# Local attention in a two-layer decoder trunk: counts of keys added to the mask as logarithms, sums of exponentials taken by ScalarE, one head of each pair scaled by VectorE

## The chip, the cores and the metric

The kernel runs on one core of one Trainium2 chip. The metric is the device time in microseconds (us); lower is better. The engines are TensorE (PE in the rows, PEld for its weight loads), VectorE (DVE), ScalarE (ACT), GpSimd (POOL) and SyncE (SP). ns is nanoseconds.

## The reference

Two layers, each with a hybrid token mixer, a cross-attention and a gated convolutional feed-forward part, on 256 tokens of width 1024. The change touches one part of the mixer, the dilated window attention of 8 heads of 64 columns:

```
DL_PATTERN = ((128, 1), (512, 4), (2048, 16))
def dilated_branch(q, k, v, window, dilation):
    ...
    s = jnp.where(valid, s, -jnp.inf)
    m = jnp.max(s, axis=-1, keepdims=True)
    p = jnp.exp(s - m)
    den = jnp.sum(p, axis=-1, keepdims=True)
    o = jnp.einsum('brhnqk,brhnkc->brhnqc', (p / den).astype(v.dtype), vw)
    lse = (m + jnp.log(den))[..., 0]
...
    wts = jax.nn.softmax(jnp.stack(lses, axis=-1), axis=-1)
    o = jnp.einsum('bshn,nbshc->bshc', wts, jnp.stack(outs, axis=0).astype(jnp.float32))
```

Three branches with different windows are merged by their softmax denominators. That merge equals one softmax over all keys in which a key that lies in n of the branches (n is 0, 1, 2 or 3) counts n times.

## The kernel before

The whole trunk is written out by hand, engine by engine; every engine runs its own list in order and the lists are tied by semaphores (`Signal` objects; `own.link` makes VectorE wait for its own last instruction). All weights pass through as 512 KB groups in a ring of four. ScalarE makes the high part of a group (`whi`, line 569), VectorE the low part (`wlo`, line 996), both in `split_group`; TensorE multiplies with both. `split(g)` means "all groups up to g". The numbers of the groups (`G_SBQK`, `G_SBV` and so on) give the order in which TensorE uses them.

Local attention comes as four pairs of heads, c = 0 to 3, r = 0 or 1 within a pair. Queries lie on the partitions: token tile 0 has 128 columns of keys and tile 1 has 256, so a head is a 128x128 piece and a 128x256 piece, 384 columns (`AW`) together. Its buffers are `sms[c % 2][r]`, those of even pairs in `arena`, those of odd pairs in `V`. The mask `negm` (0 or -3e38) and the counts `mult` (0 to 3) are 384 columns each in the constants `cst`, which are loaded once and serve both layers. The steps of a pair are:

1. TensorE, `dl_scores(c)` (lines 1796 and 1797): scores into the PSUM banks `psAB[r]`. Head r of pair c waits for `nb_ready` of head r of pair c - 1, because that is when the bank is free.
2. VectorE, `scores_max(c)` (lines 1235, 1237, 1240): adds the mask, copies the scores to `sms` and takes the row's maximum, a reduction that the trace shows as a custom instruction and an accumulator read for each piece; then the negated scaled maximum, which signals `nb_ready`.
3. ScalarE, `exp_pair(c)` (line 689): exponentials in place, signals `exp_done`.
4. VectorE, `probabilities(c)` (lines 1250, 1253): multiplies by `mult` with a running sum, then the reciprocal, which signals `den_ready`.
5. ScalarE, `scale_pair(c)` (line 698): multiplies both heads by the reciprocals, signals `p_ready`.
6. TensorE, `dl_flip(c)` (line 1598): transposes into `psCD`; ScalarE copies it out (`p_columns`, line 706), TensorE multiplies with the values (`dl_values`, lines 1808 and 1809).

TensorE's list puts one weight group between these steps, so its order around the change is: `dl_scores(0)`, group `G_SBQK`, `dl_scores(1)`, group `G_SBQK + 1`, `dl_flip(0)`, `dl_scores(2)`, group `G_SBQK + 2`, `dl_values(0)`, `dl_flip(1)`, `dl_scores(3)`, and so on. VectorE's list there is:

```
                split(G_DLV + 3 + AHEAD)
                dve.wait_ge(cst_in.sem, 16)
                scores_max(0)
                split(G_SBQK + AHEAD)
                probabilities(0)
                scores_max(1)
                split(G_SBQK + 1 + AHEAD)
                probabilities(1)
                scores_max(2)
```

Of the kernel before, what the change touches and what calls it, by code (L numbers as in the profile page):

```python
# [145 lines left out]
def hybrid_trunk(nc, x, mem, pos, consts, gains, params, pw, stream, out):  # L146
    with ExitStack() as ctx:
# [222 lines left out]
        den_ready = signal("den_ready", DL_HEADS)  # L370
        p_ready = signal("p_ready", DL_HEADS)
        p_tr = signal("p_tr", DL_HEADS)
# [48 lines left out]
        def st(i, n=1):  # L421
            return stat[:, i:i + n]
# [130 lines left out]
        def _(act):  # L553
# [54 lines left out]
            for l in range(DEPTH):  # L608
# [75 lines left out]
                def exp_pair(c):  # L684
                    for r in range(2):
                        act.wait_ge(nb_ready.sem, nb_ready.at(l, 2 * c + r + 1))
                        for q, (a, b) in enumerate(((0, P), (P, AW))):
                            p = sms[c % 2][r][:, a:b]
                            e = act.activation(p, p, ACT.Exp, bias=st(S_NB + 4 * (c % 2) + 2 * r + q),
                                               scale=HD ** -0.5)  # L690
                        e.then_inc(exp_done.sem, 1)

                def scale_pair(c):
                    for r in range(2):
                        act.wait_ge(den_ready.sem, den_ready.at(l, 2 * c + r + 1))
                        for q, (a, b) in enumerate(((0, P), (P, AW))):
                            p = sms[c % 2][r][:, a:b]
                            e = act.activation(p, p, ACT.Copy, scale=st(S_RDEN + 4 * (c % 2) + 2 * r + q))
                        e.then_inc(p_ready.sem, 1)

# [85 lines left out]
                exp_pair(0)  # L786
                scale_pair(0)
                split(G_SBQK + 1 + AHEAD)
                exp_pair(1)
                split(G_SBQK + 2 + AHEAD)  # L790
                p_columns(0)
                scale_pair(1)
                exp_pair(2)
                split(G_SBQK + 3 + AHEAD)
                mixed_hi(4, o_done, 1, attended)
                p_columns(1)
                scale_pair(2)
                exp_pair(3)
# [3 lines left out]
                transposed_in(sbT.rearrange("p c n -> p (c n)"), [a[:, :] for a in accs[0]], G_SBQK + PER_TILE, sbT_in)  # L802
                scale_pair(3)
                mixed_hi(6, o_done, 3, attended)
# [177 lines left out]
        def _(dve):  # L982
# [113 lines left out]
            for l in range(DEPTH):  # L1096
# [132 lines left out]
                def scores_max(c):  # L1229
                    w = 4 * (c % 2)  # L1230
                    for r in range(2):
# [4 lines left out]
                        for q, (a, b) in enumerate(((0, P), (P, AW))):  # L1236
# [4 lines left out]
                                          None, ALU.mult).then_inc(nb_ready.sem, 1)  # L1241

                def probabilities(c):

                    w = 4 * (c % 2)
                    for r in range(2):
                        dve.wait_ge(exp_done.sem, exp_done.at(l, 2 * c + r + 1))
                        for q, (a, b) in enumerate(((0, P), (P, AW))):
                            p = sms[c % 2][r][:, a:b]
                            e = dve.tensor_tensor_reduce(p, p, mult[:, a:b], 1.0, 0.0, ALU.mult, ALU.add,  # L1250
                                                         st(S_DEN + w + 2 * r + q))
                        own.link(e)
                        dve.reciprocal(st(S_RDEN + w + 2 * r, 2), st(S_DEN + w + 2 * r, 2)).then_inc(den_ready.sem, 1)

                def mixed_lo(n, chunk, src, bias=None):
# [114 lines left out]
                split(G_DLV + 3 + AHEAD)  # L1370
                dve.wait_ge(cst_in.sem, 16)
                scores_max(0)
                split(G_SBQK + AHEAD)
# [217 lines left out]
        def _(pe):  # L1591
# [44 lines left out]
            for l in range(DEPTH):  # L1636
# [162 lines left out]
                def dl_flip(c):  # L1799
                    for r in range(2):  # L1800
                        pe.wait_ge(p_ready.sem, p_ready.at(l, 2 * c + r + 1))
                        flip(psCD[r], sms[c % 2][r], 3).then_inc(p_tr.sem, 1)
# [452 lines left out]
```

## Time and profile before

| | |
|---|---|
| median of 3 runs | 817.45 us (816.84 to 817.47) |
| the profiled execution | 817.97 us, of which span 815.8 us from first to last instruction |
| PE busy | 807.4 us, 99% |
| DVE busy | 653.9 us, 80% |
| ACT busy | 528.3 us, 65% |
| POOL busy | 29.3 us, 4% |
| TensorE's granted clock | 1.000 (full speed) |

Shares are of the span. Matmuls overlap in the trace and their ends are modelled, so two neighbouring PE rows are best compared by their starts. Local attention lies at about 72 to 104 us in the first layer and 470 to 503 us in the second.

### The profile page before, as it was taken

How to read it: one execution, taken by the hardware profiler on the slowest of the kernel's cores; microseconds unless marked ns; L12 is line 12 of the kernel's file. 1: busy time of each engine (PE TensorE's matmuls, PEld its weight loads, DVE VectorE, ACT ScalarE, POOL GpSimd, SP SyncE). 2: the span in 40 equal slices, each digit the busy share in tenths (PEclk: the TensorE clock that was granted, in tenths of full speed). 3: DMA queues.
4: the chain of work that ended last, by engine and by line, in shares of the span. 5: the costliest groups of instructions: out<-in, count | busy, mean ns of one | idle time of the engine just before them, and what ended most of it. 6: DMA issues, size and time to landing. Idle time of an engine off the chain costs nothing.

```text
span 815.8 us, 12147 instructions
## 1 busy us (share of the span) xinstructions
PE 807.4 (99%) x4636; PEld 698.2 (86%) x4636; DVE 653.9 (80%) x1149; ACT 528.3 (65%) x823; POOL 29.3 (4%) x54
## 2 busy tenths in 40 slices
PE   8999999999999999999999999999999999999997
PEld 5998888889888888888899889888998888888885
DVE  6899996778776899997387999948788489999753
ACT  5656886567657777765365589756767477776441
POOL 2100000010010000000010000001000000000000
PEclk9999999999999999999999999999999999999999
DMA  8765345472574465556666453456635545655651
GB/s 300 285 180 182 96 137 168 143 258 95 168 242 141 157 205 204 179 187 218 193 205 231 151 155 104 136 175 204 209 114 196 181 130 181 202 174 191 231 182 52
DMA packets 40446, 145.72 MB, mean 179 GB/s; under 512 B 4594, under 2 KB 4738, under 8 KB 40388
## 3 DMA queue, kind: packets, MB, share of 16 engines
q1 hardware_dynamic: 38448, 138.38, 52.1%
q0 software_dynamic: 1936, 6.55, 2.3%
q8 instruction: 37, 0.61, 0.3%
q14 instruction: 21, 0.17, 0.1%
q10 hardware_dynamic: 4, 0.00, 0.0%
HBM read 143.87 MB, written 1.05 MB: 178 GB/s over the span
## 4 chain that ended last, share of the span: by engine, by line
PE 96%; DVE 2%; issue 1%; ACT 1%; DMA 0%; DVEq 0%; POOLq 0%; POOL 0%; ACTq 0%
PE acc L1685 8%; PE acc L1651 5%; PE acc L1652 5%; PE acc L1653 5%; PE psCD L1685 4%; PE acc L1695 4%; PE acc L1668 4%; PE acc L1748 4%; PE psAB L1685 4%; PE acc L1750 4%; PE acc L1749 4%; PE acc L1669 3%; PE acc L1670 3%; PE psAB L1651 3%; PE psAB L1652 3%; PE psAB L1653 3%
## 5 line engine op out<-in xcount | busy, mean ns | idle before, releaser
L996 DVE TENSOR_TENSOR wlo<-raw,whi 128x1024 fp32r<-128x1024 f32 x240 | 288.0, 1222 | 68.3 <-ACT whi L569 66.7
L569 ACT ACTIVATE whi<-raw 128x1024 fp32r<-128x1024 f32 x240 | 249.7, 1058 | 119.4 <-PE acc L1653 43.6
L1685 PE MATMUL acc<-xT,whi 128*128 128x512 f32 x288 | 89.0, 390 | 0.0
L1685 PEld LDWEIGHTS acc<-xT,whi 128*128 128x128 f32 x288 | 54.1, 188 | 11.8
L1539 DVE SCALAR_TENSOR_TENSOR KT<-V,par,KT 128x255 f32<-128x255 f32 (+1 forms) x144 | 60.0, 480 | 2.1 <-ACT KT L929 1.5
L1695 PE MATMUL acc<-xT,wlo 128*128 128x256 f32 x288 | 58.0, 283 | 0.0
L1276 DVE SCALAR_TENSOR_TENSOR arena<-arena,par 128x256 f32<-128x256 f32 x120 | 50.3, 482 | 0.8 <-ACT arena L769 0.8
L1668 PE MATMUL acc<-xT,whi 128*128 128x256 f32 x176 | 50.9, 289 | 0.0
L1685 PE MATMUL psCD<-xT,whi 128*128 128x512 f32 x160 | 50.0, 393 | 0.0
L1669 PE MATMUL acc<-xT,whi 128*128 128x256 f32 x176 | 49.7, 283 | 0.0
L1670 PE MATMUL acc<-xT,wlo 128*128 128x256 f32 x176 | 49.7, 282 | 0.0
L496 POOL TENSOR_TENSOR stat<-stat 128x1 f32<-128x1 f32 x30 | 18.8, 628 | 771.5 <-DVE stat L1136 400.7
L1695 PEld LDWEIGHTS acc<-xT,wlo 128*128 128x128 f32 x288 | 44.8, 191 | 0.0
L1685 PE MATMUL psAB<-xT,whi 128*128 128x512 f32 x128 | 39.7, 391 | 0.0
L929 ACT ACTIVATE KT<-V,par 128x256 f32<-128x256 f32 x72 | 37.4, 596 | 0.6 <-DVE V L1525 0.6
L1668 PEld LDWEIGHTS acc<-xT,whi 128*128 128x128 f32 x176 | 33.6, 191 | 2.9 <-issue 2.7
L619 ACT ACTIVATE junk<-acc 128x512 bf16<-128x512 f32 x20 | 11.8, 592 | 37.0 <-PE acc L1769 22.5
L1651 PE MATMUL psAB<-whi,gT 128*128 128x512 f32 x88 | 34.2, 389 | 0.0
L1652 PE MATMUL psAB<-wlo,gT 128*128 128x512 f32 x88 | 34.2, 389 | 0.0
L1653 PE MATMUL psAB<-whi,gT 128*128 128x512 f32 x88 | 34.2, 389 | 0.0
L1669 PEld LDWEIGHTS acc<-xT,whi 128*128 128x128 f32 x176 | 33.7, 191 | 0.1
L1670 PEld LDWEIGHTS acc<-xT,wlo 128*128 128x128 f32 x176 | 33.6, 191 | 0.0
(336 smaller groups left out, 2084.0 us busy)
## 6 DMA issues: line engine op xcount, KB each, us to landing
raw<-stream_dram SPq DMA_DIRECT2D x256, 512.0 KB, 4.2
gpost<-gain_dram POOLq DMA_DIRECT2D x6, 512.0 KB, 5.2
gpre<-gain_dram POOLq DMA_DIRECT2D x5, 512.0 KB, 5.9
memn<-mem_dram SPq DMA_DIRECT2D x2, 512.0 KB, 10.0
out_dram<-h SPq DMA_DIRECT2D x4, 256.0 KB, 2.1
cst<-const_dram SPq DMA_DIRECT2D x1, 896.0 KB, 6.3
h<-x_dram SPq DMA_DIRECT2D x2, 256.0 KB, 3.0
h<-x_dram SPq DMA_DIRECT2D x1, 512.0 KB, 7.4
```

The source lines that it names most:

```text
L569: act.activation(home(g)[0], raw[:, s * GW:(s + 1) * GW], ACT.Copy).then_inc(w_hi.sem, 1)
L996: dve.tensor_tensor(lo, raw[:, cols], hi.bitcast(F32), ALU.subtract).then_inc(w_lo.sem, 1)
L1276: e = dve.scalar_tensor_tensor(acc, src, w, acc, ALU.mult, ALU.add)
L1539: e = dve.scalar_tensor_tensor(y[:, c, shift:SEQ], u[:, 0:SEQ - shift], par[:, PC_FW + 3 * fc + 1 - k:PC_FW + 3 * fc + 2 - k], y[:, c, shi ...
L1651: pe.matmul(outs[t], a_hi, whi[:, cols], start=k == 0, stop=False)
L1652: pe.matmul(outs[t], a_hi, wlo[:, cols], start=False, stop=False)
L1653: e = pe.matmul(outs[t], a_lo, whi[:, cols], start=False, stop=k == k_of - 1)
L1668: pe.matmul(dst, whi[:, cols], hi[:, toks], start=k == 0 and c % 2 == 0, stop=False)
L1669: pe.matmul(dst, whi[:, cols], lo[:, toks], start=False, stop=False)
L1670: e = pe.matmul(dst, wlo[:, cols], hi[:, toks], start=False, stop=k == KC - 1 and c % 2 == 1)
L1685: e = pe.matmul(up_halves(j, c), whi[:, cols], both, start=k == 0, stop=k == KC - 1)
L1695: e = pe.matmul(up_halves(j, c)[:, 0:SEQ], wlo[:, cols], hi, start=False, stop=False)
```

## The change

The counts leave the work of every pair. In the first layer only, before the first maximum, VectorE turns the counts into 8 times their logarithm (8 undoes the score scale) by a quadratic through 0 at count 1, and adds this to the mask `negm`. From then on the exponential itself holds the count. ScalarE sums the exponentials as it makes them (`accum_out`), VectorE takes only the reciprocals, ScalarE scales head 0 of a pair and VectorE scales head 1. `p_ready` becomes two signals.

```diff
@@ ScalarE
                             p = sms[c % 2][r][:, a:b]
-                            e = act.activation(p, p, ACT.Exp, bias=st(S_NB + 4 * (c % 2) + 2 * r + q),
-                                               scale=HD ** -0.5)
+                            n = 4 * (c % 2) + 2 * r + q
+                            e = act.activation(p, p, ACT.Exp, bias=st(S_NB + n), scale=HD ** -0.5,
+                                               accum_out=st(S_DEN + n))
                         e.then_inc(exp_done.sem, 1)
...
-                def scale_pair(c):
-                    for r in range(2):
-                        act.wait_ge(den_ready.sem, den_ready.at(l, 2 * c + r + 1))
-                        for q, (a, b) in enumerate(((0, P), (P, AW))):
-                            p = sms[c % 2][r][:, a:b]
-                            e = act.activation(p, p, ACT.Copy, scale=st(S_RDEN + 4 * (c % 2) + 2 * r + q))
-                        e.then_inc(p_ready.sem, 1)
+                def scale_first(c):
+                    act.wait_ge(den_ready.sem, den_ready.at(l, 2 * c + 1))
+                    for q, (a, b) in enumerate(((0, P), (P, AW))):
+                        p = sms[c % 2][0][:, a:b]
+                        e = act.activation(p, p, ACT.Copy, scale=st(S_RDEN + 4 * (c % 2) + q))
+                    e.then_inc(p0_ready.sem, 1)
@@ VectorE
+                def log_counts():
+
+                    two, three = float(HD ** 0.5 * np.log(2.0)), float(HD ** 0.5 * np.log(3.0))
+                    bend = three / 2 - two
+                    rise = sms[1][0]
+                    own.link(dve.tensor_scalar(rise, mult, bend, two - 2 * bend, ALU.mult, ALU.add))
+                    own.link(dve.scalar_tensor_tensor(rise, mult, -1.0, rise, ALU.add, ALU.mult))
+                    own.link(dve.tensor_tensor(negm, negm, rise, ALU.add))
+
                 def probabilities(c):
 
                     w = 4 * (c % 2)
                     for r in range(2):
                         dve.wait_ge(exp_done.sem, exp_done.at(l, 2 * c + r + 1))
-                        for q, (a, b) in enumerate(((0, P), (P, AW))):
-                            p = sms[c % 2][r][:, a:b]
-                            e = dve.tensor_tensor_reduce(p, p, mult[:, a:b], 1.0, 0.0, ALU.mult, ALU.add,
-                                                         st(S_DEN + w + 2 * r + q))
-                        own.link(e)
                         dve.reciprocal(st(S_RDEN + w + 2 * r, 2), st(S_DEN + w + 2 * r, 2)).then_inc(den_ready.sem, 1)
+                    dve.wait_ge(den_ready.sem, den_ready.at(l, 2 * c + 2))
+                    for q, (a, b) in enumerate(((0, P), (P, AW))):
+                        p = sms[c % 2][1][:, a:b]
+                        e = dve.tensor_scalar(p, p, st(S_RDEN + w + 2 + q), None, ALU.mult)
+                    e.then_inc(p1_ready.sem, 1)
...
                 dve.wait_ge(cst_in.sem, 16)
+                if not l:
+                    log_counts()
                 scores_max(0)
@@ TensorE
-                        pe.wait_ge(p_ready.sem, p_ready.at(l, 2 * c + r + 1))
+                        p_ready = p1_ready if r else p0_ready
+                        pe.wait_ge(p_ready.sem, p_ready.at(l, c + 1))
```

TensorE's list keeps its order. VectorE's and ScalarE's lists change at the places below (line numbers after the change are 1 to 12 higher; ISA is the custom instruction and its accumulator read).

VectorE in the first layer, ahead of the first maximum, before:

```order
L1276 SCALAR_TENSOR_TENSOR arena<-arena,par 128x256 x4
L996 TENSOR_TENSOR wlo<-raw,whi 128x1024
L1235 MEMSET stat 128x2
L1237 ISA arena,stat<-psAB,cst 128x128
L1237 ISA stat 128x1
```

and with the change:

```order
L1286 SCALAR_TENSOR_TENSOR arena<-arena,par 128x256 x4
L997 TENSOR_TENSOR wlo<-raw,whi 128x1024
L1249 TENSOR_SCALAR V<-cst 128x384
L1250 SCALAR_TENSOR_TENSOR V<-cst,V 128x384
L1251 TENSOR_TENSOR cst<-cst,V 128x384
L1236 MEMSET stat 128x2
```

Three instructions of 384 columns now stand between the last weight split and the first maximum. In the second layer this place is as before.

VectorE, the probabilities of pair 0 behind a weight split, before, head 0:

```order
L996 TENSOR_TENSOR wlo<-raw,whi 128x1024
L1250 ISA arena,stat<-arena,cst 128x128
L1250 ISA stat 128x1
L1250 ISA arena,stat<-arena,cst 128x256
L1250 ISA stat 128x1
L1253 RECIPROCAL stat<-stat 128x2
```

(the same five instructions follow for head 1, then the MEMSET of the next maximum) and with the change:

```order
L997 TENSOR_TENSOR wlo<-raw,whi 128x1024
L1258 RECIPROCAL stat<-stat 128x2 x2
L1262 TENSOR_SCALAR arena<-arena,stat 128x128
L1262 TENSOR_SCALAR arena<-arena,stat 128x256
L1236 MEMSET stat 128x2
```

Eight instructions went, two came, in each of the four pairs of both layers.

ScalarE, exponentials of head 1 and scaling of both heads of pair 0, before:

```order
L689 ACTIVATE arena<-arena,stat 128x128
L689 ACTIVATE arena<-arena,stat 128x256
L698 ACTIVATE arena<-arena,stat 128x128
L698 ACTIVATE arena<-arena,stat 128x256
L698 ACTIVATE arena<-arena,stat 128x128
L698 ACTIVATE arena<-arena,stat 128x256
L569 ACTIVATE whi<-raw 128x1024
```

and with the change:

```order
L691 ACTIVATE arena,stat<-arena,stat 128x128
L691 ACTIVATE arena,stat<-arena,stat 128x256
L699 ACTIVATE arena<-arena,stat 128x128
L699 ACTIVATE arena<-arena,stat 128x256
L570 ACTIVATE whi<-raw 128x1024
```

The exponentials have a second output (`stat`), and one head's scaling is gone.

## Rows read from the trace of the kernel before

**Rows 1.** The page: span and busy time of the engines.

```profile
span 815.8 us, 12147 instructions
...
PE 807.4 (99%) x4636; PEld 698.2 (86%) x4636; DVE 653.9 (80%) x1149; ACT 528.3 (65%) x823; POOL 29.3 (4%) x54
```

**Rows 2.** TensorE's waits: total us, times, longest; the longest of four rows.

```profile
PE acc L1623 <- POOL idle L499: 1.4, 1, 1.4
```

**Rows 3.** Timeline of TensorE, first layer: start, length, line.

```profile
72.65 0.50 PE L1796 MATMUL psAB<-arena 64*128 64x128 f32 x4
...
73.51 0.39 PE L1668 MATMUL acc<-xT,whi 128*128 128x256 f32 x1
...
76.58 0.53 PE L1796 MATMUL psAB<-arena 64*128 64x128 f32 x3
...
77.58 0.38 PE L1668 MATMUL acc<-xT,whi 128*128 128x256 f32 x1
...
80.56 0.82 PE L1598 MATMUL psCD<-cst,arena 128*128 128x128 f32 x6
81.31 0.50 PE L1796 MATMUL psAB<-arena 64*128 64x128 f32 x4
```

**Rows 4.** Timeline of VectorE, first layer.

```profile
74.81 0.06 DVE L1235 MEMSET stat<- 128x2 f32 x1
...
75.60 0.17 DVE L1240 TENSOR_SCALAR stat<-stat 128x2 f32<-128x2 f32 x1
...
76.51 0.17 DVE L1240 TENSOR_SCALAR stat<-stat 128x2 f32<-128x2 f32 x1
...
77.72 0.29 DVE L1250 CUSTOM_DVE_ANT_0 arena<-arena,cst 128x128 f32<-128x128 f32 x1
...
79.25 0.06 DVE L1235 MEMSET stat<- 128x2 f32 x1
...
80.95 0.17 DVE L1240 TENSOR_SCALAR stat<-stat 128x2 f32<-128x2 f32 x1
```

**Rows 5.** Timeline of TensorE, second layer.

```profile
474.71 0.49 PE L1796 MATMUL psAB<-arena 64*128 64x128 f32 x2
...
475.62 0.48 PE L1796 MATMUL psAB<-arena 64*128 64x128 f32 x2
...
476.47 0.38 PE L1668 MATMUL acc<-xT,whi 128*128 128x256 f32 x1
```

**Rows 6.** Timeline of VectorE, second layer; in brackets idle before it.

```profile
449.28 2.56 DVE L1276 SCALAR_TENSOR_TENSOR arena<-arena,par 128x256 f32<-128x256 f32 x6 [0.77 <-ACT arena L769]
...
475.40 0.17 DVE L1240 TENSOR_SCALAR stat<-stat 128x2 f32<-128x2 f32 x1
```

**Rows 7.** Timeline of VectorE at 36 us and 64 us: chains linked by semaphore.

```profile
36.90 0.23 DVE L1020 TENSOR_SCALAR arena<-arena 128x128 f32<-128x128 f32 x1
37.16 0.95 DVE L1026 SCALAR_TENSOR_TENSOR arena<-arena 128x128 f32<-128x128 f32 x3
...
64.81 0.42 DVE L1226 TENSOR_TENSOR arena<-arena 128x256 f32<-128x256 f32 x1
```

**Rows 8.** Groups by line and shape: busy us, mean ns | idle us before.

```profile
L1467 DVE TENSOR_SCALAR arena<-arena,stat 128x256 f32<-128x256 f32 x16 | 4.9, 351 | 0.3
L1293 DVE SCALAR_TENSOR_TENSOR arena<-arena 128x768 f32<-128x768 f32 x4 | 3.8, 958 | 1.9 <-ACT arena L723 1.9
...
L1036 DVE TENSOR_SCALAR xn<-memn,stat 128x1024 f32<-128x1024 f32 x2 | 1.5, 746 | 0.0
```

**Rows 9.** Timeline of ScalarE: attention pair 0, and cross-attention.

```profile
76.10 1.50 ACT L689 ACTIVATE arena<-arena,stat 128x128 f32<-128x128 f32 x4
78.59 1.55 ACT L698 ACTIVATE arena<-arena,stat 128x128 f32<-128x128 f32 x4 [0.99 <-DVE stat L1253]
...
190.44 0.47 ACT L855 ACTIVATE arena<-psAB,stat 128x256 f32<-128x256 f32 x1
190.79 0.20 ACT L855 ACTIVATION_READ_ACCUMULATOR arena<-psAB,stat 128x1 f32 x1
```

More of the change, by code:

```diff
@@ L370, in hybrid_trunk @@
         den_ready = signal("den_ready", DL_HEADS)
-        p_ready = signal("p_ready", DL_HEADS)
+        p0_ready = signal("p0_ready", DL_HEADS // 2)
+        p1_ready = signal("p1_ready", DL_HEADS // 2)
         p_tr = signal("p_tr", DL_HEADS)
@@ L786, in _ @@
                 exp_pair(0)
-                scale_pair(0)
+                scale_first(0)
                 split(G_SBQK + 1 + AHEAD)
@@ L791, in _ @@
                 p_columns(0)
-                scale_pair(1)
+                scale_first(1)
                 exp_pair(2)
@@ L796, in _ @@
                 p_columns(1)
-                scale_pair(2)
+                scale_first(2)
                 exp_pair(3)
@@ L802, in _ @@
                 transposed_in(sbT.rearrange("p c n -> p (c n)"), [a[:, :] for a in accs[0]], G_SBQK + PER_TILE, sbT_in)
-                scale_pair(3)
+                scale_first(3)
                 mixed_hi(6, o_done, 3, attended)
```

## The prediction

> **What bounds the kernel now.** I read the page first, then TensorE's waits, then the timelines of TensorE and VectorE side by side. The page shows TensorE busy for 807.4 of 815.8 us [rows 1], VectorE and ScalarE well below. The table of TensorE's waits has four rows only, the longest 1.4 us and at the very start of the program [rows 2]. So TensorE's own list is the time: work taken from VectorE or ScalarE buys nothing unless TensorE stands waiting for it, and whatever makes TensorE wait longer is added to the end in full, because nothing behind it is idle that could take it up.
>
> A wait shorter than a matmul's modelled length doesn't show as idle time, so I compared starts. The score products of a pair cost TensorE 0.86 us when nothing holds them: pair 0 starts at 72.65, the next weight group at 73.51 [rows 3]. Pair 1 of the first layer takes 1.00 us (76.58 to 77.58), and in the second layer 1.76 us (474.71 to 476.47), with head 1 starting only at 475.62 [rows 3, 5]. What holds it is VectorE: the instruction that frees the bank of head 1 ends at 475.40 + 0.17 = 475.57, 0.05 us before head 1 starts, and the next group follows 0.85 us after that start [rows 5, 6]. The first layer obeys the same sum: VectorE ends at 76.51 + 0.17 = 76.68, plus 0.05, plus 0.85, gives 77.58, and that is the row [rows 3, 4]. So in both layers TensorE already waits for VectorE at `dl_scores(1)`, by 0.14 us in the first and 0.90 us in the second. This is the one place of the attention where VectorE sets the end.
>
> **The change part by part.**
>
> *The logarithm of the counts.* Three VectorE instructions of 384 columns go in ahead of the first maximum, first layer only, each followed by a wait for itself. No row has 384 columns, so I go between rows. The TENSOR_SCALAR with constants took 0.23 us at 128 columns [rows 7]; the two rows with a scalar from memory, 351 ns at 256 and 746 ns at 1024 columns, give (746 - 351)/768 = 0.51 ns a column [rows 8]; 0.23 + 256 x 0.51 ns = 0.36 us. The SCALAR_TENSOR_TENSOR: three at 128 columns in 0.95 us with two gaps are 0.29 each [rows 7], and 958 ns at 768 columns [rows 8] gives 1.04 ns a column; 0.29 + 256 x 1.04 ns = 0.56 us. The TENSOR_TENSOR: 0.42 at 256 columns [rows 7], plus 128 x 1.04 ns = 0.55 us. The gap of a self-wait is 37.16 - 36.90 - 0.23 = 0.03 us [rows 7], three times 0.09. Sum: 0.36 + 0.56 + 0.55 + 0.09 = **1.56 us**. From below: 256 columns for all three, 0.35 + 0.42 + 0.42 + 0.09 = 1.28 us. From above: the first at 1.04 ns a column (0.50), the other two as long as the 768-column row (0.96 each), 0.09: 2.51 us. I take 1.56, since 384 columns lie far nearer to the rows at 256 than to that at 768.
>
> For this price there is a rule in the Trainium skill, page "VectorE: DVE Perf Modes", section on the TRN2 errata: an SBUF to SBUF operation takes 58 cycles plus columns divided by the mode's factor, at 0.96 GHz. By its figures the three would be an estimated 0.26, 0.46 and 0.46 us, 1.27 us with the gaps, and the time 818.7 us. The trace doesn't agree: a TENSOR_TENSOR of 256 columns took 0.42 us [rows 7] where that formula has 0.33. The same section's other formula, (N + 151) cycles, has 0.42 and agrees.
>
> *Who waits for it.* VectorE has no idle time there: the first maximum began at 74.81 directly behind a weight split [rows 4] and the head-1 signal at 76.68 is already the late one. Both `nb_ready` signals of pair 0 move by 1.56 us, `dl_scores(1)` of the first layer with them, and everything behind it. TensorE pays 1.56 us, once. In the second layer nothing stands ahead of the first maximum that wasn't there, and VectorE's position there doesn't descend from the first layer: it still stood idle for 0.77 us at 449.28, waiting for ScalarE [rows 6]. The second layer's 0.90 us stays.
>
> *VectorE's pairs.* Multiply-and-sum and reciprocals of a pair take from 77.72 to 79.25, 1.53 us [rows 4]. Now: two reciprocals, about 0.25 us together (0.17 for an instruction of two columns, the second overlapping [rows 4]), a gap of 0.03, then scalings of 128 and 256 columns, 0.29 and 0.35 us by the rows above [rows 8]: 0.92. That is 0.6 us less in each of 8 pairs, 4.9 us of VectorE time. None of it is on TensorE's path: pair 1's head-1 signal ended at 80.95 + 0.17 = 81.12 [rows 4], while TensorE started that pair's successor at 81.31 and reached head 1 at half of 0.86 later, 81.74 [rows 3]. A margin of 0.6 us becomes 1.2. Cost and gain: nothing.
>
> *ScalarE.* An exponential with a sum is followed by an accumulator read. In cross-attention the read starts 0.35 us into the activation and ends at 0.55, where the activation alone ends at 0.47 [rows 9]: 0.08 us more, for four of them 1.50 + 0.32 = 1.8 us a pair. From above: the reads not overlapped, 4 x 0.20, 2.3 us. The scaling falls from 1.55 [rows 9] to 0.78. A pair costs ScalarE 0.45 us less, or at worst the same. Covered.
>
> *The transposes.* `dl_flip(0)` at 80.56 [rows 3] followed the end of the scaling at 78.59 + 1.55 = 80.14 [rows 9] by 0.42 us. With the change TensorE comes at 82.12. Head 1's exponentials start when its signal comes, 76.68 + 1.56 = 78.24, and take half of 1.8: 79.1. The split ends at 77.72 + 1.56 = 79.28; reciprocals to 79.5; ScalarE's head 0 to 80.3, VectorE's head 1 to 80.2. The margin grows to 1.8 us. If that cover were gone, each late 0.1 us would count eight times.
>
> **Sum.** Profiled execution 817.97 + 1.56 = 819.53 us, of which 815.8 + 1.56 = 817.4 span. The median stands 0.52 us below the profiled execution, so 817.45 + 1.56 = **819.0 us**, 0.19% more. What a measurement of this kernel can tell from no change is about 0.2%, 1.63 us: the forecast lies just inside it.
>
> **The rivals.**
>
> *A. Only part of the delay arrives (no change).* It needs the 0.14 us of the first layer to be TensorE's own and not a wait for head 1. Then only head 0 counts: its signal ended at 75.60 + 0.17 = 75.77, plus 0.05, against TensorE's 76.58 [rows 3, 4], a margin of 0.76. The cost is 1.56 - 0.76 = 0.80 us, 818.25. For it: 0.14 us is small. Against it: the sum 0.05 + 0.85 meets both layers to a hundredth.
>
> *B. Faster.* The mechanism would be that VectorE, at 80% the second busiest, and not TensorE, sets the pace through the attention, with waits hidden in the modelled matmul lengths. Then the 0.6 us of each pair come out of the time: 817.45 + 1.56 - 8 x 0.6 = 814.2 us. It decides once TensorE's hidden waits in the pairs reach 1.56 us beyond those that the first signal sets. Against it: pair 2's score products take from 81.31 on with a margin of 0.6 us, and the transposes have 0.42.
>
> *C. Clearly slower.* VectorE's second reciprocal now waits for the exponentials of head 1 with their accumulator reads, and behind it in VectorE's list stands the maximum of the next pair, for which TensorE's scores of the pair after that wait. The margin there is 0.6 + 0.6 = 1.2 us. If exponentials with sums from and to SBUF ran at 3.3 us a pair instead of 1.8, VectorE would come 1.5 late, 0.3 us over the margin, at three pairs of two layers: 1.8 us, 817.45 + 1.56 + 1.8 = 820.8 us. For it: no row shows this form of exponential with a sum, that of cross-attention reads PSUM. Against it: even unoverlapped reads give 2.3 us, short of what it needs.
>
> **How the numbers follow.** Forecast 0.74, A 0.10, B 0.03, C 0.13. The forecast's own range is 1.28 to 2.51 us of cost, 818.7 to 820.0, with the 0.3 us by which medians wander 818.4 to 820.3. The range that takes A in, and leaves B and the far part of C out, is 817.7 to 820.4. Faster by over 0.2% is B, 0.03. Of the forecast about 0.42 of its chance lies above 819.08 (a cost over 1.63 us needs only 0.07 us more than the sum), 0.31; with C that makes slower 0.44. The rest of the forecast and A make same 0.53.
>
> **What the profile of the changed kernel would show.** Three rows of VectorE in the first layer, V<-cst, V<-cst,V and cst<-cst,V, of about 0.36, 0.56 and 0.55 us, first maximum at about 76.4 instead of 74.81. In TensorE's timeline pair 1 of the first layer starting near 77.4, not 76.58, and the weight group after it at 79.1, not 77.58; now long enough to appear in the table of waits. In the second layer the same pair with head 1 again 0.91 us behind head 0. TensorE's busy time as before. VectorE's busy time less by some 4 us, ScalarE's by some 3. A is right if the group comes near 78.4. C is right if VectorE waits for ScalarE ahead of a reciprocal for a microsecond or so and `dl_scores(2)` shows a gap. The prediction is wrong if a wait appears at the transposes, at a weight group or in the second layer.

## The result, and the profile after

| | before | after |
|---|---|---|
| median us | 817.66 (816.84 to 817.89, 11 runs) | 819.39 (818.61 to 820.97, 11 runs) |
| ratio | | 1.0023, 95% interval 1.0015 to 1.0031 |
| span of the profiled execution | 815.8 | 816.9 |
| DVE busy us | 653.9 | 649.5 |
| ACT busy us | 528.3 | 525.1 |

The change costs 1.73 us, between 1.2 and 2.5. The forecast was 819.0; on the 11 runs of the kernel before, its 1.56 us come to 819.22.

The page of the changed kernel, its span and busy times, beside [rows 1]:

```profile
span 816.9 us, 12118 instructions
...
PE 808.0 (99%) x4636; PEld 698.4 (85%) x4636; DVE 649.5 (80%) x1104; ACT 525.1 (64%) x839; POOL 29.3 (4%) x54
```

VectorE lost 4.4 us of work and ScalarE 3.2 us, and the span grew by 1.1 us. TensorE's waits have the old first row of [rows 2] and this new one behind it:

```profile
PE psAB L1808 <- DVE stat L1241: 0.7, 1, 0.7
```

TensorE's timeline of the changed kernel in the first layer, beside [rows 3]. L1808 begins the score products of a pair, L1680 a weight group, L1610 the transposes:

```profile
72.22 0.50 PE L1808 MATMUL psAB<-arena 64*128 64x128 f32 x4
...
73.08 0.39 PE L1680 MATMUL acc<-xT,whi 128*128 128x256 f32 x1
...
76.94 0.48 PE L1808 MATMUL psAB<-arena 64*128 64x128 f32 x2 [0.73 <-DVE stat L1241]
...
77.85 0.49 PE L1808 MATMUL psAB<-arena 64*128 64x128 f32 x2
...
78.70 0.38 PE L1680 MATMUL acc<-xT,whi 128*128 128x256 f32 x1
...
81.67 0.82 PE L1610 MATMUL psCD<-cst,arena 128*128 128x128 f32 x6
...
82.42 0.39 PE L1808 MATMUL psAB<-arena 64*128 64x128 f32 x2
```

I measure the stretch from the start of pair 0's score products to the group behind pair 1's. Before it was 77.58 - 72.65 = 4.93 us [rows 3], now 78.70 - 72.22 = 6.48: 1.55 us more. The span grew by less, because the first score product came 0.43 us earlier, 72.22 instead of 72.65: 1.55 - 0.43 = 1.12. That difference arises at the start of the program; over the profiled executions of this study the first score product wandered between 71.6 and 73.2.

VectorE's timeline there, beside [rows 4]:

```profile
74.35 0.35 DVE L1249 TENSOR_SCALAR V<-cst 128x384 f32<-128x384 f32 x1
74.73 0.56 DVE L1250 SCALAR_TENSOR_TENSOR V<-cst,V 128x384 f32<-128x384 f32 x1
75.32 0.56 DVE L1251 TENSOR_TENSOR cst<-cst,V 128x384 f32<-128x384 f32 x1
75.95 0.06 DVE L1236 MEMSET stat<- 128x2 f32 x1
...
76.72 0.17 DVE L1241 TENSOR_SCALAR stat<-stat 128x2 f32<-128x2 f32 x1
...
77.63 0.17 DVE L1241 TENSOR_SCALAR stat<-stat 128x2 f32<-128x2 f32 x1
...
78.84 0.22 DVE L1258 RECIPROCAL stat<-stat 128x2 f32<-128x2 f32 x2
79.09 0.55 DVE L1262 TENSOR_SCALAR arena<-arena,stat 128x128 f32<-128x128 f32 x2
79.59 0.06 DVE L1236 MEMSET stat<- 128x2 f32 x1
...
81.29 0.17 DVE L1241 TENSOR_SCALAR stat<-stat 128x2 f32<-128x2 f32 x1
```

From the first row of the logarithm to the first MEMSET are 1.60 us. Head 0's signal ends at 76.72 + 0.17 = 76.89 and TensorE starts at 76.94; head 1's at 77.80, TensorE at 77.85. Both follow by the 0.05 us of the prediction. A pair's probabilities now take 78.84 to 79.59, 0.75 us.

In the second layer the same three rows of TensorE as [rows 5] read:

```profile
475.79 0.49 PE L1808 MATMUL psAB<-arena 64*128 64x128 f32 x2
...
476.70 0.48 PE L1808 MATMUL psAB<-arena 64*128 64x128 f32 x2
...
477.55 0.38 PE L1680 MATMUL acc<-xT,whi 128*128 128x256 f32 x1
```

Head 1 still comes 0.91 us behind head 0, and 1.76 us lie between head 0 and the group, as before.

ScalarE's timeline of pair 0, beside [rows 9], three of its nine rows:

```profile
76.92 0.40 ACT L691 ACTIVATE arena<-arena,stat 128x128 f32<-128x128 f32 x1 [1.27 <-DVE stat L1241]
...
78.63 0.19 ACT L691 ACTIVATION_READ_ACCUMULATOR arena<-arena,stat 128x1 f32 x1
79.03 0.80 ACT L699 ACTIVATE arena<-arena,stat 128x128 f32<-128x128 f32 x2 [0.21 <-DVE stat L1258]
```

Four exponentials with their sums end at 78.82, 1.90 us. The scaling ends at 79.83 and the transposes start at 81.67, 1.84 us later.

### The profile page after: what moved, and what is told of

It is laid out like the page before. It is cut to its first block, busy times and chain, and to the rows that moved or that the text cites. A ratio compares the mean times of both kernels' runs of the same rounds, so it can differ in the third digit from the quotient of the medians.

```text
span 816.9 us, 12118 instructions
## 1 busy us (share of the span) xinstructions
PE 808.0 (99%) x4636; PEld 698.4 (85%) x4636; DVE 649.5 (80%) x1104; ACT 525.1 (64%) x839; POOL 29.3 (4%) x54
## 3 DMA queue, kind: packets, MB, share of 16 engines
HBM read 143.87 MB, written 1.05 MB: 177 GB/s over the span
## 4 chain that ended last, share of the span: by engine, by line
PE 93%; DVE 4%; issue 1%; DMA 1%; ACT 1%; SPq 0%; DVEq 0%; POOLq 0%; POOL 0%
PE acc L1697 8%; PE psCD L1697 4%; PE acc L1663 4%; PE acc L1664 4%; PE acc L1665 4%; PE acc L1707 4%; PE acc L1760 4%; PE psAB L1697 4%; PE acc L1762 4%; PE acc L1761 4%; PE acc L1680 4%; PE psAB L1664 3%; PE psAB L1663 3%; PE psAB L1665 3%; PE acc L1681 3%; PE acc L1682 3%
## 5 line engine op out<-in xcount | busy, mean ns | idle before, releaser
L1680 PE MATMUL acc<-xT,whi 128*128 128x256 f32 x176 | 50.9, 289 | 0.0
L1680 PEld LDWEIGHTS acc<-xT,whi 128*128 128x128 f32 x176 | 33.6, 191 | 2.9 <-issue 2.7
```

Of the source, the lines that this page charges most:

```text
L1680: pe.matmul(dst, whi[:, cols], hi[:, toks], start=k == 0 and c % 2 == 0, stop=False)
```

## The experiments

For each kernel I took the starts of TensorE's score products and weight groups from its timeline. This table is worked out from those starts, in us. A stretch is that of above; with no wait for VectorE it is 0.86 + 3.07 + 0.86 = 4.79, and so it was read in four of the kernels. The kernel before was measured anew beside each group of experiments, and each ratio is to those runs: 817.86 beside e1 to e4, 817.11 beside e5 to e8, 817.62 beside e9 to e12. The expectations give times from 819.39 or from one of the earlier values, so they are best compared by their differences.

```
kernel                          layer 1  layer 2   ratio to before [95%]
before                            4.93     5.84
after                             6.48     5.84    1.0023 [1.0015, 1.0031]
e1  no logarithm                  4.90     5.82    0.9998 [0.9989, 1.0007]
e2  before + logarithm            6.47     5.83    1.0024 [1.0014, 1.0034]
e3  logarithm in both layers      6.44     7.38    1.0053 [1.0040, 1.0065]
e4  two taps moved back           4.88     4.79    0.9993 [0.9984, 1.0002]
e5  three taps moved back         4.79     4.79    0.9994 [0.9985, 1.0003]
e6  before + three taps back      4.79     4.79    1.0013 [1.0004, 1.0022]
e7  logarithm three times        10.32     5.83    1.0094 [1.0080, 1.0107]
e8  logarithm on GpSimd           5.87     5.82    1.0030 [1.0019, 1.0042]
e9  VectorE scales both heads     6.47     5.83    1.0021 [1.0012, 1.0030]
e10 ScalarE scales both heads     6.49     5.83    1.0022 [1.0013, 1.0031]
e11 logarithm early               5.52     5.83    1.0009 [1.0000, 1.0018]
e12 early + three taps back       4.79     4.79    0.9984 [0.9975, 0.9993]
```

**e1 and e2: each half of the change alone.** e1 takes the call out of the changed kernel, which leaves the keys' counts out of the result. e2 puts the same three instructions, with their output in an unused buffer, into the kernel before.

```diff
@@ e1, of the changed kernel
-                if not l:
-                    log_counts()
@@ e2, of the kernel before: the log_counts of the change, all three
@@ results into rise, an unused buffer
+                if not l:
+                    log_scratch()
                 scores_max(0)
```

> The changed kernel without the three instructions of log_counts: the counts of the keys are left out of the softmax, all else as changed. My theory (the whole cost is the three instructions ahead of the first maximum, and the rebalanced pairs are free): the span of the first layer's two score products, from pair 0's start to the weight group after pair 1, falls back from 6.48 us to 4.93 us, and the time is that of the kernel before, about 817.7 us. The rival that the pairs cost time as well (accumulator reads, VectorE's new wait at the reciprocal): 4.93 us too, but the rest of the attention longer than before, and a time of 818.2 us or more. The rival that the pairs gain time (VectorE as hidden bound): below 816.5 us.

> The kernel before, with the same three instructions of 384 columns ahead of the first maximum of the first layer, their result put into a scratch buffer instead of the mask; the pairs as before. My theory: the cost is theirs alone, 6.48 us from pair 0 to the group after pair 1 where the kernel before has 4.93, and a time of 817.66 + 1.55 = 819.2 us. With the old, longer pairs the margin at pair 2's scores shrinks no further than 0.6 us, since TensorE is late by the same amount. The rival that the pairs carry part of the cost: less than 818.6 us. The rival that they hid part of it: above 820 us.

e1: 817.63 (816.75 to 818.05, 11 runs) against 817.86. e2: 819.61 (818.99 to 820.65, 8 runs). The stretch moves with the three instructions alone, by 1.58 us between e1 and the changed kernel and 1.54 between before and e2. The rest of the change, alone in e1, moves no start of TensorE at the score products, counted from pair 0's, by more than 0.05 us, and its time is that of the kernel before to within 0.9 us.

**e3: the price in a second place.** The scratch version of the three instructions in the second layer of the changed kernel as well.

```diff
                 if not l:
                     log_counts()
+                else:
+                    log_scratch()
```

> The changed kernel, with three more instructions of the same shapes at the same place in the second layer (into scratch, the mask stays). My theory: VectorE already sets TensorE's pace at that place in the second layer, so another 1.55 us arrive in full: pair 0's start to the group after pair 1 goes from 5.84 to 7.39 us in the second layer, and the time to 819.39 + 1.55 = 820.9 us. The rival that only what exceeds head 0's margin arrives gives the same in this layer, as there is no margin for head 0; a rival in which the delay is taken up later (weight groups, transposes) gives less than 820.2 us.

822.14 (820.71 to 822.64, 5 runs). The second layer's stretch grew by 1.54 us, as expected; the time is 1.2 us above the 820.9 that I had expected. The execution that was profiled is the 820.71 one, 1.8 us above the profiled 818.92 of the changed kernel; in the four others the mean granted clock was 0.996 to 0.997, where the changed kernel mostly has 0.998 to 0.999. That extra is not the wait, whose length is in the profile. e7 looks for it; for these four executions themselves no profile was taken.

**e4: make room at the place.** Two filter taps, four VectorE instructions of 0.4 us, go from ahead of the first maximum to behind it. (The expectations call each of these instructions a tap.)

```diff
-                conv_taps(13, 15)
                 split(G_DLV + 3 + AHEAD)
...
                 scores_max(0)
+                conv_taps(13, 15)
```

> The changed kernel with the four convolution taps of conv_taps(13, 15) moved, in both layers, from ahead of the last weight split to right behind the first maximum; everything is still computed. Four taps take 1.58 us. My theory: the maximum comes 1.58 us earlier in both layers. In the first layer that cancels the logarithm (1.55), leaving pair 0's start to the group after pair 1 at about 4.9 us (now 6.48); in the second the wait of 1.05 us (5.84 against 4.79 without any wait) goes away. Together 1.6 + 1.05 = 2.6 us: 819.39 - 2.6 = 816.8 us, below the kernel before. The rival that order within VectorE's list doesn't matter, only its total: 819.4 us. A rival in which the taps, now later, delay the maximum of pair 1: a new wait at the third score product, up to 1.6 us of the gain lost in each layer.

817.17 (816.59 to 817.69, 11 runs). The stretch is 1.60 us shorter than after the change in the first layer and 1.05 in the second, but part came back at the third score product: 80.24 to 81.76, 1.52 us instead of 0.86, and 0.97 in the second layer. Moved back by one pair only, the work is late for the next: of the 2.65 us, 0.77 were lost again, as the last rival of the expectation had it in part.

**e5 and e6: three taps (six instructions, 2.46 us) further back, with the change and without it.**

```diff
-                conv_taps(11, 13)
+                conv_taps(11, 12)
...
-                conv_taps(13, 15)
...
                 scores_max(1)
+                conv_taps(12, 15)
```

> The changed kernel with six taps (conv_taps(12, 15)) moved, in both layers, from ahead of the first maximum to behind the maximum of pair 1; everything is computed. With four taps behind the maximum of pair 0, VectorE's maximum of pair 1 became what TensorE waits for: the third score product took 1.52 and 0.97 us instead of 0.86. My theory: behind pair 1 they delay neither, so all score products of both layers take 0.86 us and the group after pair 1 comes 4.79 us after pair 0 (now 6.48 and 5.84). Against the kernel before that is 0.14 + 1.05 = 1.2 us less: 816.6 us. The rival that the taps now hold the maximum of pair 2: its margin was about 2 us and the total of VectorE's work ahead of it is unchanged, so it would need 2 us; then 817.5 us or more.

> The kernel before, without the change, with the same six taps moved behind the maximum of pair 1. My theory: the whole gain is a matter of order on VectorE and needs nothing of the change, so this too has all score products at 0.86 us, 4.79 us from pair 0 to the group after pair 1 in both layers, and 817.86 - 1.2 = 816.7 us. The rival that the change's shorter pairs are needed to make room: a new wait at the fourth score product or at a transpose, and a time at least 0.3 us above that of e5_six_behind_pair1.

e5: 816.63 (816.01 to 817.26, 11 runs), e6: 818.32 (817.52 to 818.91, 11 runs), on one chip with 817.11 for before. In both the first two pairs run without any wait, which is worth 0.14 + 1.05 = 1.19 us. But e5 is only 0.48 us below the kernel before, and its interval includes no change: I had expected 1.2 us less, and that its time came near the expected 816.6 is luck, as the kernel before was 0.75 us faster here than beside e1. My expectation for e6 was wrong too, and the rival right: it is 1.21 us above the kernel before. The timelines show why. TensorE's fourth score products in e6:

```profile
86.75 0.49 PE L1796 MATMUL psAB<-arena 64*128 64x128 f32 x2
...
87.25 0.37 PE L1796 MATMUL psAB<-arena 64*128 64x128 f32 x1
```

VectorE in e6 ahead of them, the first maximum of pair 0, then pair 1's probabilities and pair 2's maxima:

```profile
73.74 0.06 DVE L1235 MEMSET stat<- 128x2 f32 x1 [1.27 <-PE psAB L1797]
...
83.79 0.28 DVE L1250 CUSTOM_DVE_ANT_0 V<-V,cst 128x128 f32<-128x128 f32 x1
...
85.33 0.06 DVE L1235 MEMSET stat<- 128x2 f32 x1
...
87.03 0.17 DVE L1240 TENSOR_SCALAR stat<-stat 128x2 f32<-128x2 f32 x1
```

TensorE's fourth score products in e5:

```profile
85.95 0.50 PE L1808 MATMUL psAB<-arena 64*128 64x128 f32 x4
```

VectorE in e5 ahead of them:

```profile
83.24 0.22 DVE L1258 RECIPROCAL stat<-stat 128x2 f32<-128x2 f32 x2
83.49 0.55 DVE L1262 TENSOR_SCALAR V<-V,stat 128x128 f32<-128x128 f32 x2
83.99 0.06 DVE L1236 MEMSET stat<- 128x2 f32 x1
...
85.68 0.17 DVE L1241 TENSOR_SCALAR stat<-stat 128x2 f32<-128x2 f32 x1
```

In e6 the probabilities of pair 1 take 83.79 to 85.33, 1.54 us, head 1's signal ends at 87.20, and head 1 starts at 87.25, 0.50 behind head 0: the product takes 1.35 us. In e5 they take 0.75 us, the signal ends at 85.85, and the product runs through in 0.87.

Why is VectorE late in e6, where only the order of its work has changed? Without the taps it is ready for pair 0 before TensorE has made the scores, and stands idle for 1.27 us at 73.74, where the kernel before had none. The taps come later in full. Counted from the start of pair 0, pair 2's head-1 signal ends at 87.20 - 72.69 = 14.51 us in the first layer. In the kernel before it ends at 85.67 - 72.65 = 13.02, by this row of VectorE:

```profile
85.50 0.17 DVE L1240 TENSOR_SCALAR stat<-stat 128x2 f32<-128x2 f32 x1
```

e6 pays once more ahead of pair 2's products with the values. The weight group there takes 3.38 us in both layers, where the kernel before has 3.04 and e5 3.25 and 3.04. The start of those products in the second layer of e6:

```profile
494.83 0.66 PE L1808 MATMUL acc<-arena 128*64 128x256 f32 x4 [0.27 <-ACT arena L706]
```

This wait is for ScalarE's copy of the transposes, and ScalarE had come to it from scaling both heads of the pair, 1.54 us instead of 0.80. So a part of what the change buys here may be ScalarE's saved work, not VectorE's, and no run separates the two. At the next products into `psAB` another 0.17 us are lost. With the 0.49 us of the fourth score products e6 loses 1.0 us in each layer, against the 1.19 gained in both together: 0.8 us more than before by the profiles, 1.21 by the medians. e5 loses 0.37 us in the first layer, at the last two places, and 0.04 in the second: 0.8 us less than before by the profiles, 0.48 by the medians. The differences of 0.4 and 0.3 us stay open. These are the only places where the change's shorter pairs were seen to buy time: e5 is 1.69 us below e6, though it carries the logarithm.

**e7: more of the wait.** log_scratch() twice more behind log_counts() of the first layer. If only the wait costs, this adds two more of it; if TensorE's idling costs clock as well, more.

```diff
                 if not l:
                     log_counts()
+                    log_scratch()
+                    log_scratch()
```

> The changed kernel with the three instructions done three times at the same place of the first layer (the extra ones into scratch). 3.1 us more of VectorE ahead of the first maximum, so TensorE stands idle for about 3.8 us there. The theory that only the wait counts: 819.39 + 3.1 = 822.5 us. The rival, from e2_log_alone's trace, that TensorE's idle time also costs granted clock afterwards (there one stretch of 3.4 us at half clock behind the wait, and the weight group after pair 1 took 4.47 us instead of 2.97): the clock falls here in every execution, the group after pair 1 takes 4.5 us or more, and the time is 824 us or more.

825.05 (824.45 to 825.15, 4 runs), mean clock 0.995 in all. Busy time and granted clock in stretches of e7 (columns: stretch, length, busy us and count of PE, PEld, DVE, ACT and POOL, clock, DMA share, GB/s):

```profile
70.00:76.50 6.50, 6.38 (x43) 5.15 (x41) 6.36 (x13) 4.51 (x6) 0.00 (x0) 1.00 0.66 182
76.50:80.00 3.50, 0.00 (x0) 0.00 (x0) 3.23 (x11) 0.00 (x0) 0.00 (x0) 1.00 0.27 111
80.00:81.00 1.00, 0.78 (x4) 0.56 (x4) 0.91 (x8) 0.80 (x3) 0.00 (x0) 0.83 0.00 0
81.00:87.00 6.00, 6.00 (x26) 5.22 (x25) 5.35 (x23) 4.59 (x17) 0.00 (x0) 0.50 0.36 96
```

TensorE stood idle for 3.84 us, took up work at 80.22, and then ran at 0.50, the 1.2 GHz level, for over 6 us. The score product took 2.48 us instead of 1.76 and the group behind it 5.07 instead of 2.97: 2.8 us on top of the wait. The theory that only the wait counts is refuted, and the rival with its 824 us or more holds. The same after a short wait, in e2's profiled execution, its slowest run:

```profile
70.00:78.00 8.00, 7.28 (x48) 5.73 (x48) 7.70 (x23) 5.32 (x10) 0.00 (x0) 1.00 0.62 195
78.00:79.50 1.50, 1.50 (x10) 1.17 (x9) 1.47 (x7) 0.42 (x2) 0.00 (x0) 0.85 0.00 0
79.50:82.50 3.00, 3.00 (x16) 3.00 (x16) 2.79 (x18) 3.00 (x7) 0.00 (x0) 0.51 0.56 180
82.50:86.00 3.50, 3.50 (x31) 3.00 (x31) 3.29 (x21) 3.50 (x10) 0.00 (x0) 1.00 0.52 137
```

TensorE had idled 0.72 us before 76.69; the group of 78.44 then took 4.47 instead of 2.97 us. In the changed kernel's profiled execution the same wait was followed by full clock, the group 2.97. So the wait carries a second price of 1.5 us that falls due in some executions only.

**e8: the logarithm on another engine.** GpSimd computes it, in four instructions, as soon as the constants are in; VectorE waits for it ahead of the first maximum, 40 us later.

```diff
@@ GpSimd, its semaphores left out
+            pool.tensor_scalar(less, mult, 1.0, -1.0, ALU.mult, ALU.add)
+            pool.tensor_scalar(rise, mult, bend, two - 2 * bend, ALU.mult, ALU.add)
+            pool.tensor_tensor(rise, less, rise, ALU.mult)
+            pool.tensor_tensor(negm, negm, rise, ALU.add)
@@ VectorE
-                if not l:
-                    log_counts()
+                dve.wait_ge(counts_in.sem, 4)
```

> The changed kernel with the logarithm of the counts made by GpSimd, which is idle there, as soon as the constants have arrived (four instructions instead of three, since one is split in two); VectorE only waits for the result. My theory: VectorE's maximum starts where it did before the change, the group after pair 1 comes 4.95 us after pair 0, and the time is 817.8 us, the kernel before. The rival that GpSimd slows VectorE's or its own later work, or comes too late: a wait of VectorE ahead of the first maximum, or longer VectorE rows while GpSimd runs, and 818.5 us or more.

819.74 (819.11 to 820.24, 6 runs) against 817.11. GpSimd's timeline in e8, the last two of its four instructions:

```profile
31.24 1.33 POOL L528 TENSOR_TENSOR V<-V 128x384 f32<-128x384 f32 x1
32.65 1.35 POOL L530 TENSOR_TENSOR cst<-cst,V 128x384 f32<-128x384 f32 x1
```

VectorE's timeline in e8 beside them:

```profile
30.71 2.41 DVE L1062 TENSOR_TENSOR mT_lo<-xn,mT_hi 128x512 fp32r<-128x512 f32 x2
33.05 2.10 DVE L1056 TENSOR_TENSOR xn<-memn,mem_cols 128x512 f32<-128x512 f32 x2
```

The same two rows of VectorE in the kernel before:

```profile
30.97 1.28 DVE L1049 TENSOR_TENSOR mT_lo<-xn,mT_hi 128x512 fp32r<-128x512 f32 x2
32.17 1.29 DVE L1043 TENSOR_TENSOR xn<-memn,mem_cols 128x512 f32<-128x512 f32 x2
```

They are 1.13 + 0.81 = 1.94 us longer beside GpSimd, more than the 1.55 us that were taken off VectorE. It stayed late up to the attention, where the stretch is 0.94 us over that of before. TensorE had paid for it twice before, with a start 0.45 us and one 0.39 us later against the kernel before:

```profile
49.84 0.50 PE L1674 MATMUL acc<-whi,xT 128*128 128x512 f32 x1 [0.20 <-DVE wlo L1009]
...
67.09 0.66 PE L1621 MATMUL psCD<-cst,arena 128*128 128x128 f32 x4 [0.17 <-DVE arena L1240]
```

That makes 1.8 us of the 2.6 by which the medians differ; where the rest lies I can't place. The expected 817.8 us was wrong, the rival that GpSimd slows VectorE right. The Trainium skill, page "SBUF — State Buffer", section "SBUF: two separate sides", has an exclusive lock on a shared port pair between GpSimd and a VectorE instruction with two SBUF inputs, held for a whole instruction. These rows agree in direction: 2.41 instead of 1.28 us.

**e9 and e10: who scales.** Both heads by VectorE, or both by ScalarE.

```diff
@@ e9, VectorE's probabilities
-                    for q, (a, b) in enumerate(((0, P), (P, AW))):
-                        p = sms[c % 2][1][:, a:b]
-                        e = dve.tensor_scalar(p, p, st(S_RDEN + w + 2 + q), None, ALU.mult)
-                    e.then_inc(p1_ready.sem, 1)
+                    for r, ready in enumerate((p0_ready, p1_ready)):
+                        for q, (a, b) in enumerate(((0, P), (P, AW))):
+                            p = sms[c % 2][r][:, a:b]
+                            e = dve.tensor_scalar(p, p, st(S_RDEN + w + 2 * r + q), None, ALU.mult)
+                        e.then_inc(ready.sem, 1)
@@ e10: the loop over r stands in ScalarE's scale_first, VectorE's scaling is gone
```

> The changed kernel with VectorE scaling both heads of a pair and ScalarE none. VectorE's pair grows from 0.75 to about 1.25 us, still under the 1.53 of before, and ScalarE loses 0.75 us a pair. My theory (the pairs are off TensorE's path, with a margin of some 1 us at the third score product): every segment of TensorE's timeline as in the changed kernel, 819.4 us. The rival that VectorE's share decides the pairs: the third or fourth score product above 0.86 us, up to 0.5 us in each of three pairs of two layers, 820 to 822 us.

> The changed kernel with ScalarE scaling both heads, as before the change, but still without the counts and with the sums taken by ScalarE; VectorE keeps two reciprocals a pair. My theory: again nothing moves on TensorE, 819.4 us; the exponentials with sums cost ScalarE 0.3 us more a pair than before, inside the margin at the transposes. The rival that accumulator reads make ScalarE the late engine: a wait at the transposes (0.75, 0.81, 0.63 and 0.57 us long now), and 820 us or more.

e9: 819.40 (818.81 to 819.92, 11 runs); e10: 819.17 (818.60 to 820.01, 11 runs); before 817.62. In neither did a score product or a transpose wait that didn't before; e10's profiled execution again had the half-clock stretch after the wait (group 4.48 us).

**e11 and e12: the logarithm where VectorE has nothing to do.** In e11 it goes to 39 us, ahead of a wait for ScalarE (0.54 us idle, and 0.26 behind it). e12 has the tap order of e5 too. It computes all that the reference asks for.

```diff
@@ e11
+                if not l:
+                    dve.wait_ge(cst_in.sem, 16)
+                    log_counts()
                 dve.wait_ge(cv_sig.sem, cv_sig.at(l, 1))
...
-                if not l:
-                    log_counts()
                 scores_max(0)
```

> The changed kernel with log_counts moved on VectorE from ahead of the first maximum to about 36 us earlier, ahead of VectorE's wait for ScalarE's sigmoid, where it stood idle for 0.54 and then 0.26 us. My theory: what matters is how late VectorE is at the maximum; of the 1.56 us some 0.8 are taken up by that idle time and the rest still arrives, as VectorE is busy without a gap from there to the maximum. The group after pair 1 comes about 5.7 us after pair 0 (6.48 as changed, 4.93 before), 818.6 us. The rival that it is free there: 4.93 us and 817.8 us. The rival that the position doesn't matter: 6.48 and 819.4.

> Both moves: log_counts ahead of the wait for the sigmoid, and six taps behind the maximum of pair 1 in both layers. Everything is computed. My theory: the score products of both layers wait for nothing (4.79 us), and VectorE, earlier by 0.8 us in the first layer than in e5_six_behind_pair1, no longer holds what follows pair 3 there. 1.2 us below the kernel before and 2.9 below the changed one, a ratio of 0.9985 to the kernel before. The rival that ScalarE holds the values of pair 2 or the stick-breaking scores whatever VectorE does: like e5_six_behind_pair1, 0.9994.

e11: 818.43 (817.76 to 819.41, 11 runs). e12: 816.50 (815.57 to 816.99, 11 runs) against 817.62, less than both kernels: 0.16% under before, with an interval (0.9975 to 0.9993) that lies wholly below 1. 1.12 us less were measured, 1.2 expected; the rival, a time like e5's, is refuted, and the group ahead of pair 2's values takes 3.04 us again in both layers. VectorE of e11; the row at 41.15 had 0.54 us of idle time before it in the kernel before and has none now:

```profile
39.58 0.35 DVE L1249 TENSOR_SCALAR V<-cst 128x384 f32<-128x384 f32 x1
...
41.15 0.69 DVE L1352 TENSOR_TENSOR arena<-acc,arena 128x512 f32<-128x512 f32 x1
```

Of 1.55 us, 5.52 - 4.93 = 0.59 still reach TensorE, where the expected 5.7 leave 0.77. In e12 no product waits, 4.79 us in both layers.

## Why the prediction was right

**Place and mechanism.** TensorE already waited for VectorE at `dl_scores(1)`, hidden in the lengths of the matmuls, and three instructions ahead of that wait came through in full. The group at 78.70 and both 0.05 us distances are as forecast: with the program's start 0.43 us earlier, 78.70 stands for 79.13, where 79.1 was forecast. e1 and e2 show that the three instructions by themselves are the whole of it.

**Size.** 0.35, 0.56 and 0.56 us against 0.36, 0.56 and 0.55; 1.55 us in the stretch against 1.56. The rule of the Trainium skill, page "VectorE: DVE Perf Modes", by which it would have been an estimated 1.27 us isn't borne out.

**What was worth nothing.** The second layer stayed at 5.84, the transposes had 1.84 us to spare (forecast 1.8), and e9 and e10 moved work between the two engines without moving TensorE. The exponentials of a pair take 1.90 us (forecast 1.8).

**The term that was off.** The probabilities of a pair take 0.75 us, not 0.92: I added a gap to two scalings end to end, 0.29 + 0.35, and they overlap to 0.55; two reciprocals take 0.22. It was on no path.

**The rivals.** A (part of the delay): refuted, 1.55 us arrived. B (VectorE's shorter pairs count): refuted for this order by e1, where they stand alone and the time is that of before; e5 against e6 shows that in another order they do count. C (reciprocals late): refuted, the exponentials with sums took 1.90 us, not the 3.3 that it needed, VectorE's reciprocals at 78.84 followed the weight split without idle time, and head 1's signal of pair 1 ended at 81.46, while TensorE began at 82.42.

**What I did not foresee.** The medians differ by 1.73 us where the stretch gives 1.55. Two of the 11 runs (820.67 and 820.97) have a mean clock of 0.997 and 0.996. A stretch at half clock after the wait, which costs 1.5 us, would lift them by about as much as they lie above the others, and the profiles of e2, e7 and e10 show such stretches; for those two runs themselves no profile was taken, so that part is argued, not shown. It doesn't explain the median either: without the two runs it would be 819.32, 0.07 us less. The 0.18 us lie within the interval.

**Same or slower.** The prediction called 1.63 us the least that can be told from no change, put its 1.56 just inside, and gave "same" 0.53 and "slower" 0.44. The measured 1.73 us lies just outside, with an interval wholly above 1. The mechanism doesn't decide between the two; a tenth of a microsecond does, and on which side it fell is chance.

**Where VectorE's gain went.** Its 4.4 us lie behind the one wait that TensorE has for it in this order, and e5 against e6 shows what it takes for them to count. My expectation for e6 took a move within VectorE's list to be free of cost behind the place where it helps. Two things ate that margin at the fourth score product. In the first layer TensorE came only 0.13 us sooner, but VectorE 1.49 us later, since it had stood idle where the taps had been. In the second layer TensorE came 1.03 us sooner, because its wait of 1.05 us was gone, and VectorE 0.56 later.

## What to carry to other kernels

Work done once still costs its full length if it stands ahead of the one wait that sets the end; it belongs into that engine's idle time, and e11 got 0.96 of the 1.55 us back by that, e12, with the taps moved as well, all of it. Find such a wait by comparing starts of matmul groups with an unhindered one: the 0.90 us of the second layer showed no idle time in the profile. When work is moved behind a wait, the margins further on shrink from both sides: the engine that waited comes sooner, and the engine that does the work comes later, by as much as it now stands idle ahead of it. Work them out anew before moving it.

## What the runs showed of the hardware

- The granted clock fell from 2.4 to the 1.2 GHz level behind an idle TensorE. After 3.84 us idle it was at 0.50 from 81 to 87 us. After 0.7 us it fell in the profiled executions of e2 (for over 3 us) and e10, and did not in those of the changed kernel, e3 and e9, nor after the 1.63 us that TensorE stood idle in e3's second layer.
- VectorE's pair of 128x512 TENSOR_TENSOR took 2.41 instead of 1.28 us beside GpSimd's TENSOR_TENSOR of 384 columns, which took 1.33.
- The read of ScalarE's accumulator took 0.19 us but overlaps: four exponentials with their reads took 1.90 us, against 1.50 without [rows 9].
